# Layer 1's up projection begun on X times g, ahead of its norm, with four weight splits on GpSimd

## What is computed

```
x = x + gt1 * mixer_output(...)                       # out projection, gated residual
h = x * rsqrt(mean(x*x) + EPS) * g_ffn                # norm of 1024 channels
h = h * (1 + sc2) + sh2                               # modulation by the condition
a, b = split(h @ w_up)                                # 1024 -> 2 x 2816
x = x + gt2 * ((silu(dwconv3(a) + bias) * b) @ w_down)
```

## Time and profile before

| | us |
|---|---|
| three timed runs | 1293.45, 1293.62, 1295.55 |
| their median | 1293.62 |
| the profiled execution | 1291.46 |
| its span in the profile | 1289.70 |
| PE busy | 1258.4 (98% of the span) |
| DVE busy | 877.9 (68%) |
| ACT busy | 554.2 (43%) |
| POOL busy | 301.8 (23%) |

### The profile page before, as it was taken

One profiled execution on the slowest core, in us unless ns is written; L12 is line 12 of the kernel. 1 busy time (PEld: TensorE's weight loads), 2 busy tenths in 40 slices (PEclk: granted clock), 3 DMA queues, 4 the chain that ended last, 5 costly groups with the idle time before them and its releaser, 6 DMA issues.

```text
span 1289.7 us, 19927 instructions
## 1 busy us (share of the span) xinstructions
PE 1258.4 (98%) x7682; PEld 1090.1 (85%) x7682; DVE 877.9 (68%) x1184; ACT 554.2 (43%) x874; POOL 301.8 (23%) x254
## 2 busy tenths in 40 slices
PE   5999999999999999999999999999999999999998
PEld 3788777777788798888888888998889998999998
DVE  4696778753699777663779664586786666665664
ACT  4322355554433245332223332343676645653543
POOL 0005399210132101111001110002792230220222
PEclk8999999999999999999999999999999998999999
DMA  9464511222366325663555663334433543664560
GB/s 372 175 219 151 176 62 62 74 66 67 117 200 235 125 90 179 195 201 99 175 163 190 203 212 123 106 123 155 144 119 115 185 159 131 199 223 135 188 218 34
DMA packets 49762, 198.75 MB, mean 154 GB/s; under 512 B 5520, under 2 KB 5904, under 8 KB 48528
## 3 DMA queue, kind: packets, MB, share of 16 engines
q1 hardware_dynamic: 49680, 197.62, 46.1%
HBM read 196.55 MB, written 1.05 MB: 153 GB/s over the span
## 4 chain that ended last, share of the span: by engine, by line
PE 95%; DVE 3%; issue 1%; ACT 1%; DMA 1%; SPq 0%; DVEq 0%; ACTq 0%
PE psA L532 26%; PE psA L534 26%; PE psA L533 26%; PE psB L532 2%; PE psB L534 2%; PE psB L533 2%; PE psA L771 2%; PE psB L787 2%; PE psB L799 2%; PE psB L714 1%; PE psB L553 1%; DMA X<-x 1%; DVE w_lo L1305 1%; PE psB L702 0%; ACT w_hi L986 0%
## 5 line engine op out<-in xcount | busy, mean ns | idle before, releaser
L532 PE MATMUL psA<-h_hi,w_hi 128*128 128x256 f32 (+1 forms) x1528 | 520.6, 341 | 6.3 <-DVE h_lo L1453 2.6
L533 PE MATMUL psA<-h_lo,w_hi 128*128 128x256 f32 (+1 forms) x1528 | 513.2, 336 | 0.0
L534 PE MATMUL psA<-h_hi,w_lo 128*128 128x256 f32 (+1 forms) x1528 | 513.1, 336 | 0.0
L986 ACT ACTIVATE w_hi<-raw 128x1024 fp32r<-128x1024 f32 (+2 forms) x244 | 276.9, 1138 | 286.3 <-PE psA L534 212.3
L1305 DVE TENSOR_TENSOR w_lo<-raw,w_hi 128x1024 fp32r<-128x1024 f32 (+2 forms) x244 | 337.9, 1385 | 90.5 <-ACT w_hi L986 90.3
L532 PEld LDWEIGHTS psA<-h_hi,w_hi 128*128 128x128 f32 x1528 | 291.3, 191 | 40.5 <-issue 7.2
L534 PEld LDWEIGHTS psA<-h_hi,w_lo 128*128 128x128 f32 x1528 | 291.3, 191 | 29.7
L533 PEld LDWEIGHTS psA<-h_lo,w_hi 128*128 128x128 f32 x1528 | 291.6, 191 | 28.5 <-issue 0.2
L517 POOL TENSOR_TENSOR hid_lo<-sig,hid_hi 128x512 f32 (+3 forms) x44 | 67.2, 1527 | 474.5 <-ACT hid_hi L1265 474.5
L1326 DVE SCALAR_TENSOR_TENSOR ada_sum<-raw,csil,ada_sum 128x1024 f32<-128x1024 f32 x112 | 154.6, 1412 | 0.0
L532 PE MATMUL psA<-hid_hi,w_hi 128*128 128x256 f32 (+1 forms) x352 | 116.3, 331 | 2.1 <-DVE sig L1766 2.0
(11 more groups left out here) (204 smaller groups left out, 1492.3 us busy)
## 6 DMA issues: line engine op xcount, KB each, us to landing
raw<-w_up SPq DMA_DIRECT2D x88, 512.0 KB, 4.2
raw<-w_ada SPq DMA_DIRECT2D x80, 512.0 KB, 3.6
raw<-w_dn SPq DMA_DIRECT2D x32, 704.0 KB, 4.6
raw<-w_in SPq DMA_DIRECT2D x36, 512.0 KB, 4.4
raw<-w_at SPq DMA_DIRECT2D x24, 512.0 KB, 3.5
raw<-w_fn SPq DMA_DIRECT2D x16, 640.0 KB, 4.1
raw<-w_sc SPq DMA_DIRECT2D x16, 640.0 KB, 3.9
raw<-w_cf SPq DMA_DIRECT2D x16, 640.0 KB, 4.1
```

What stands on the lines that cost most here:

```text
L532: pe.matmul(out, w0, hi, start=first, stop=False)
L533: pe.matmul(out, w0, lo, start=False, stop=False)
L534: return pe.matmul(out, w1, hi, start=False, stop=last)
L986: act.activation(w_hi[:, s, 0:tiles * P], raw[:, r, 0:tiles * P], ACT.Copy).then_inc(head_done, 1)
```

## The change

In layer 1's `up0` the first three chunks (the lead) no longer wait for the norm. In the out stage ACT and DVE also write X * g of each tile, split in two (`bare_hi`, `bare_lo`), with two more columns that hold the shift. PE multiplies the first two chunks by them as soon as `out` is done, and the third two tiles later, with the mean and the spread in between (`bare_lead`), into three banks (`lead_bank`). ACT copies the spread inverse root to SBUF (`inverse_row`), and DVE's `scaled` reads that copy. When the three chunks are read, DVE multiplies them by the inverse root and adds the shift's product (column 256, read by ACT into `lead_shift`). The norm's h is still made, for chunk 3 onward; chunk 3 waits for its tiles one by one. The weight rests of chunks 2 to 5 of `up0` are written by POOL (`beside_done`) and no longer by DVE. ACT's splits of chunks 3, 4 and 5 move to behind the root, between tiles 5 and 6 of the norm, and behind the reads of the shift's product. PE runs four more chunks outside its hardware loop. Chunks 4 and 5 don't wait for a PSUM bank.

The diff, cut to its core (`rested` corrects the count of DVE's splits where waits use it):

```diff
@@ helpers @@
+BARE = SEQ + 2
+UP1, BESIDE = PER_LAYER + START["up0"], AHEAD - 1
+def beside(n):
+    return BESIDE <= n - UP1 < 2 * AHEAD
+        inverse_row = sqb[:, SEQ:NT]
+        lead_row = [tmp[0][:, SEQ:NT], sig[0][:, SEQ:NT], tmp[1][:, SEQ:NT]]
+        lead_bank = [psB[1], psB[2], psA[(PER_LAYER + START["up0"] + 2) % SLOTS]]
@@ SP @@
-                    if item == "w":
-                        sp.wait_ge(rest_done, m + 1 + shift)
+                    if item == "w" and beside(m):
+                        sp.wait_ge(beside_done, m - UP1 - BESIDE + 1)
+                    elif item == "w":
+                        sp.wait_ge(rest_done, rested(m, not isinstance(shift, int)) + shift)
@@ POOL, ahead of hidden_rest @@
+                    if layer and f == 0:
+                        for n in range(UP1 + BESIDE, UP1 + 2 * AHEAD):
+                            p = PLACE[("w", n)]
+                            pool.wait_ge(head_done, n + 1)
+                            pool.tensor_tensor(w_lo[:, n % SLOTS, 0:KD * P], raw[:, p % SLOTS, 0:KD * P],
+                                               w_hi[:, n % SLOTS, 0:KD * P].bitcast(F32), ALU.subtract)\
+                                .then_inc(beside_done, 1)
@@ PE @@
+            def bare_lead(r):
+                sts = [Step(PER_LAYER + START["up0"] + j, j) for j in range(AHEAD)]
+                for st in sts[:-1]:
+                    begin(st)
+                for at_ in range(KD + 2):
+                    if at_ == 2:
+                        begin(sts[-1])
+                        mean_square(r, 0)
+                    if at_ == 4:
+                        spread_inverse(r, 0)
+                    if at_ < KD:
+                        pe.wait_ge(bare_rest, at_ + 2)
+                    for st in sts:
+                        kk = at_ - (2 if st is sts[-1] else 0)
+                        if 0 <= kk < KD:
+                            mm = product(lead_bank[st.idx][:, 0:BARE], st, kk, bare_hi[:, kk, :], bare_lo[:, kk, :],
+                                         kk == 0, kk == KD - 1)
+                            if kk == KD - 1:
+                                mm.then_inc(chunk_done, 1)
-                if layer:
-                    norm_stat(2 * layer + 1)
+                        if layer and f == 0 and st.idx == AHEAD:
+                            for kk in range(KD):
+                                pe.wait_ge(h_rest, 48 + kk + 1)
+                                mm = product(psA[st.slot][:, 0:T], st, kk, h_hi[:, kk, 0:T], h_lo[:, kk, 0:T],
+                                             kk == 0, kk == KD - 1)
@@ ACT @@
+            def bare(o):
+                act.activation(bare_hi[:, o, 0:SEQ], X[:, o, 0:SEQ], ACT.Copy, scale=gsc[:, 1, 0, o:o + 1])\
+                    .then_inc(bare_head, 1)
+            def covered_norm():
+                up = PER_LAYER + START["up0"]
+                norm_root(3, 0)
+                head(Step(up, 0), KD)
+                act.wait_ge(spread, normed(3, 0))
+                act.activation(inverse_row, spread_bank[0][:, 0:SEQ], ACT.Copy).then_inc(inverse_in, 1)
+                for kk in range(KD):
+                    if kk == 6:
+                        head(Step(up + 1, 1), KD)
+                    shifted_head(1, 1, 0, kk)
+                for j in range(AHEAD):
+                    act.wait_ge(chunk_done, up + j + 1)
+                    act.activation(lead_shift[:, j:j + 1], lead_bank[j][:, SEQ:SEQ + 1], ACT.Copy)\
+                        .then_inc(lead_shifted, 1)
+                head(Step(up + 2, 2), KD)
                         if st.idx:
                             square(8 * r + st.idx - 1, st.idx - 1, T, st.idx == 1, (evac, st.n))
+                            if r == 3:
+                                if st.idx == 1:
+                                    bare_shift()
+                                bare(st.idx - 1)
                         if st.idx == KD - 1:
                             last_squares(r, (evac, st.n + 1))
+                            if r == 3:
+                                bare(KD - 1)
@@ DVE @@
+            def bare_rest_of(o):
+                dve.wait_ge(bare_head, o + 2)
+                dve.scalar_tensor_tensor(bare_lo[:, o, 0:SEQ], X[:, o, 0:SEQ], gsc[:, 1, 0, o:o + 1],
+                                         bare_hi[:, o, 0:SEQ].bitcast(F32), ALU.mult, ALU.subtract)\
+                    .then_inc(bare_rest, 1)
                 dve.scalar_tensor_tensor(tmp[kk % 2][:, cols], X[:, kk, cols], gsc[:, which, s, kk:kk + 1],
-                                         spread_bank[s][:, cols], ALU.mult, ALU.mult).then_inc(ht, 1)
+                                         inverse_row if r == 3 else spread_bank[s][:, cols],
+                                         ALU.mult, ALU.mult).then_inc(ht, 1)
-                        rest(st, size(st, name))
+                        if r != 3 or not beside(st.n + AHEAD):
+                            rest(st, size(st, name))
                         op.then_inc(evac, 1)
+                        if r == 3 and st.idx:
+                            if st.idx == 1:
+                                bare_shift_rest()
+                            bare_rest_of(st.idx - 1)
@@ DVE, lift @@
+                        if layer and f == 0 and st.i is None and st.idx < AHEAD:
+                            ps = lead_row[st.idx]
+                            dve.wait_ge(chunk_done, st.n + 1)
+                            dve.wait_ge(lead_shifted, st.idx + 1)
+                            dve.tensor_tensor(ps, lead_bank[st.idx][:, 0:SEQ], inverse_row, ALU.mult)\
+                                .then_inc(lead_scaled, 1)
+                            dve.wait_ge(lead_scaled, 2 * st.idx + 1)
+                            dve.tensor_scalar(ps, ps, lead_shift[:, st.idx:st.idx + 1], None, ALU.add)\
+                                .then_inc(lead_scaled, 1)
+                            dve.wait_ge(lead_scaled, 2 * st.idx + 2)
+                        else:
+                            rest(st, size(st, f"up{f}"))
```

More of the change, by code:

```diff
@@ L282, in program @@
         mats_late = sem("mats_late")
+        bare_head, bare_rest, inverse_in, lead_shifted, lead_scaled = map(sem, (
+            "bare_head", "bare_rest", "inverse_in", "lead_shifted", "lead_scaled"))
         x_full = [sem(f"x_full{j}") for j in range(4)]
@@ L423, in load @@
                                 .then_inc(raw_full[p % SLOTS], 16)
-                    walk(sp, layer, name, load, skip=LEN[name] if layer == 0 or name == "in" else 0)
+                    walk(sp, layer, name, load, skip=LEN[name] if layer == 0 or name == "in" else 3 if name == "up0" else 0)
                     if layer == 0 and name == "cf":
@@ L536, in begin @@
             def begin(st):
-                pe.wait_ge(rest_done, st.up(st.n + 1))
-                if st.n >= SLOTS:
+                if st.i is None and beside(st.n):
+                    pe.wait_ge(beside_done, st.n - UP1 - BESIDE + 1)
+                else:
+                    pe.wait_ge(rest_done, st.up(rested(st.n, st.i is not None)))
+                free = st.i is None and st.n - UP1 in (SLOTS, SLOTS + 1)
+                if st.n >= SLOTS and not free:
                     pe.wait_ge(evac, st.up(st.n - SLOTS + 1))
@@ L920, in _ @@
                     if f == 0:
-                        lead(layer, "up0", T, KD, h_hi, h_lo, (h_rest, 16 * (2 * layer + 1)),
-                             2 * layer + 1)
-                        walk(pe, layer, "up0", lift, lead=AHEAD, skip=straight)
+                        if layer:
+                            bare_lead(2 * layer + 1)
+                        else:
+                            lead(layer, "up0", T, KD, h_hi, h_lo, (h_rest, 16), 1)
+                        walk(pe, layer, "up0", lift, lead=AHEAD, skip=straight or 2)
                     else:
@@ L1267, in lift @@
                     def lift(st):
-                        head(st, size(st, layer, f"up{f}"))
+                        covered = layer and f == 0 and st.i is None and st.idx < AHEAD
+                        if not covered:
+                            head(st, size(st, layer, f"up{f}"))
                         pair, b = st.idx // 2, (st.idx // 2) % 2
```

49 lines of the change are left out of this document (41 added, 8 removed).

## The result

| | before | after |
|---|---|---|
| median, us (22 runs each, side by side) | 1292.75 | 1296.67 |
| lowest to highest, us | 1289.95 to 1296.45 | 1292.25 to 1299.28 |
| ratio, 95% interval | | 1.0023 [1.0014, 1.0033] |
| profiled execution, us; its span | 1291.46; 1289.7 | 1296.53; 1294.7 |
| granted clock over the span | 0.995 | 0.992 |

The ratio is 3.0 us of the 1293.62 that the prediction started from, which makes 1296.6: what was forecast, 1296.6. The change makes the kernel slower by 0.23%. The interval runs from 1.8 to 4.3 us, and the two medians of the table differ by 3.9, so 3.0 is not known to a tenth.

What follows compares the result with a forecast made beforehand. PE bounds the kernel (95% of the chain), losing 7.1 us at the out-to-up edge. A 3.4 us gain without contention becomes a 3.0 us loss through POOL's holds and half clock: 1293.62 + 3.0 = 1296.6 us, range 1290.8 to 1299.0.

Steps and rivals of the forecast that it cites:

- X7 and the mean: End of out: POOL's split of up chunk 2 delays DVE's tile 7 X step to 1084.7; PE resumes at 1086.1.
- A hold at the first scaled: Start of h: POOL's split of up chunk 3 holds DVE's first scaled from 1089.35 to 1089.9, 3.8 us late.
- the rival that gets worse: Longer POOL steps or more half clock, perhaps also before the mean (up to +1.7): 1298.1 to 1299.6; chance 0.17.
- Two holds at the last two h_lo: End of h: POOL's splits of up chunks 4 and 5 hold DVE; h ends at 1101.9, up chunk 3 at 1102.3.
- Half clock behind U3: PE after up chunk 3: 18 products at half clock following its waits, costing 1.7 us.
- U6: Up chunk 6 on PE: starts 3.0 us late at 1109.75; DVE's split, ready at 1108.9, is covered by up chunk 5.
- The sum: Whole kernel: 3.0 us slower, 1293.62 + 3.0 = 1296.6 us.
- POOL's 1024 step: Each POOL weight split, 128x1024: 2.4 us, extrapolated from 0.73 at 256 wide and 1.29 at 512.
- The bound of 2.9: Upper limit for one POOL weight split running next to DVE: up to 2.9 us instead of 2.4.
- The gain without contention, 3.4 us: Edge from out to up: without POOL and DVE contention, up chunk 6 starts at 1103.4 instead of 1106.76.
- DVE steps with one input in PSUM are not held: DVE beside POOL: only steps with two SBUF inputs wait for POOL's instruction; those with one PSUM input don't.
- the change delivers: Rival: POOL runs only in DVE's pauses or holds for part of an instruction; -3.4 us, 1290.2; chance 0.17.

Runs made afterwards that it cites:

- e9: The kernel after, plus unread products on PE where it waits in the edge, and only there: 1295.0 beside 1292.56, ratio 1.0018.
- e1: The kernel after, with the four weight splits back on DVE and the lead kept: 1292.48 beside 1293.44, ratio 0.9991.
- e7: e1 with third chunk joining four tiles late, its DVE split behind tile 7's X step, Sqrt table loaded earlier: 1290.51 beside 1293.9, ratio 0.9981.
- e2: The kernel before, with only the splits of up chunks 2 to 5 moved to POOL, no lead: 1295.06 beside 1293.44, ratio 1.0006.
- e4: The kernel after, but POOL's splits of up chunks 4 and 5 wait until h is done: 1295.81 beside 1293.44, ratio 1.0014.
- e6: e1 plus four POOL steps of the same size on scratch data that nobody waits for: 1298.0 beside 1293.9, ratio 1.0045.
- e8: The kernel after, but scaled reads the spread inverse root from PSUM, not its SBUF copy: 1296.02 beside 1293.9, ratio 1.0025.

## Why the prediction was right, step by step

The mechanism held in the main: POOL's whole-instruction holds at X7 and at the last two `h_lo` take back the lead's gain, and half clock behind U3 adds to it. That the ratio gives the forecast's 3.0 to a tenth is luck: the interval is 1.8 to 4.3 us, and the one trace has 3.75, with two terms too small (h's later end and U3's last tile, 0.4 each) and the first `scaled` late for another reason than the one given.

Times of after are given less 1.0, to stand beside the prediction's.

- **X7 and the mean.** Predicted: POOL from 1081.6 to 1084.0, X7 at 1084.7, PE goes on at 1086.1. Measured: POOL 1081.3 to 1083.7, X7 1084.2, PE 1085.7. Right, and a little kinder.
- **A hold at the first scaled.** Wrong in its mechanism. POOL's split of U3 lay at 1087.2 to 1089.6 and held nobody, since the inverse row came later still: PE's first half-speed stretch (13 products at 0.215 us) put the spread at 1089.3. The first `scaled` came at 1090.6, predicted 1089.9. I had named that stretch, with up to +1.7, but only in the rival that gets worse. It hides the hold, and puts the first `scaled` 0.7 later than the hold would have. In e9, at full clock, the first two `scaled` came 1.5 earlier from the edge's start and took 1.14 instead of 0.88: the hold of U3's split is worth 0.26 there, not the 0.55 (1089.35 to 1089.9) that I gave it.
- **Two holds at the last two h_lo.** Predicted end 1101.9, U3's end 1102.3; measured 1102.26 and 1103.13. POOL got one turn ahead of each, as foreseen. U3's last tile ran at half clock, three products and a slow first one, which I hadn't priced: 0.4.
- **Half clock behind U3.** Predicted 18 products, 1.7 us; measured 21, of which 18 in U4, which took 1107.63 - 1103.13 = 4.50 instead of 2.88: 1.6.
- **U6.** Predicted 3.0 late, at 1109.75, with a DVE split ready at 1108.9 that U5 covers. Measured 1109.5 for the split and 1110.51 for U6, 3.75 late. The cover was named rightly: in e9, where the clock is full, PE comes early and waits 0.9 for exactly that split.
- **The sum.** 3.0 predicted, 3.75 in the one trace, 3.0 by the times. The difference of the trace is 0.4 from h's later end and 0.4 from U3's last tile.
- **POOL's 1024 step.** 2.4 from 0.73 and 1.29; measured 2.40 undisturbed. The bound of 2.9 fell.
- **The gain without contention, 3.4 us.** Never seen. e1 and e7 gain 1.0 and 1.8, but their DVE does the four splits that the 3.4 left to POOL. No kernel here has neither, so the figure stays an estimate.
- **DVE steps with one input in PSUM are not held.** e2's two steps of 0.48 bear it out. What I missed is that the change itself takes PSUM away from the lift chain's steps; after was spared only because its POOL pair had ended by then, and e4 paid.

The Trainium skill (SBUF — State Buffer, section "SBUF: two separate sides") has the port pair locked for a whole instruction, with the loser blocked. The trace agrees: 4.89 for 0.96 beside two POOL steps of 2.4, and 1.65 beside steps of a quarter of the size. Of the rivals, "the change delivers" fell with e6, whose holds came in full.

**What stays open:** how often, over executions, the first half-speed stretch comes, and so what the clock is worth in the median. The profile of after has it, that of e8 hasn't, and the times of e9 and after can't be told apart.

## What to carry to other kernels

Work moved to GpSimd isn't free of VectorE: list the VectorE steps that will run beside it and have all their tensors in SBUF, and charge each up to the whole length of one GpSimd instruction where it lies on the chain. If the work must go there, cut it into short instructions: here, in quarters, VectorE's steps lost 3.2 us in all instead of 5.9, and the pair on the chain 0.7 instead of 3.9. Look also at the order in which the inputs of that work become ready, since it decides beside which steps it runs (e2 against after). And when a step's input moves from PSUM to SBUF, its neighbours on GpSimd must be looked at again.

## What the runs showed of the hardware

- A waiting POOL instruction gets its turn between two DVE instructions that are ready back to back: two `h_lo` and two POOL steps alternated, 4.89 for DVE and 4.96 for POOL (after), 4.89 and 4.97 (e6). DVE never got two in a row while POOL had a step waiting.
- One tensor operand is enough to be held: `tmp<-tmp,lead_shift`, one SBUF tensor in and one out, took 2.27 beside POOL where it takes 0.35 alone (e4). Before that I had counted only steps with two SBUF tensors as held.
- PE's clock fell to 0.57 over four us in one execution and stayed at 1.00 in another whose waits were the same within 0.1 us (after and e8).
- Where DVE is there first, POOL is the one that waits: 2.4 became 3.40 beside a DVE split of 1.23 (e6).
